# The head of a two-block transformer kernel: first norm ahead of the small vectors, weight loads issued without waiting for them

## The chip, the core and the metric

The kernel runs on one core of a Trainium2 chip. The core has a matrix engine (TensorE, PE in the profile, with its weight loads as PEld), a vector engine (VectorE, DVE), a scalar engine (ScalarE, ACT), GpSimd (POOL) and a sync engine (SyncE, SP) that does nothing here but issue transfers. The engines run their own instruction streams and meet only at semaphores. Sixteen DMA engines move data between the chip's memory (HBM) and the on-chip memory (SBUF). PE writes its results into PSUM, from where DVE or ACT take them; PSUM is used here as eight banks, which the program hands out in rings.

The metric is the device time of one execution in microseconds (us). The numbers compared are medians of several executions.

## What is computed

The reference is a chain of two transformer stacks with 256 tokens of width 1024. Only the beginning matters for this change: the first layer normalizes x and multiplies it with `a_w_in`.

```python
def rmsnorm(x, g):
    xf = x.astype(jnp.float32)
    y = xf * lax.rsqrt(jnp.mean(xf * xf, axis=-1, keepdims=True) + EPS)
    return (y * g.astype(jnp.float32)).astype(x.dtype)
...
def recurrent_block(h, norm_g, w_in, conv_w, conv_b, gate_w, gate_b, lam, w_out):
    u = rmsnorm(h, norm_g)
    z = u @ w_in
    y = jax.nn.gelu(z[..., :LRU_WIDTH])
    xr = causal_conv(z[..., LRU_WIDTH:], conv_w, conv_b)
    hr = rg_lru(xr, gate_w, gate_b, lam)
    return (y * hr) @ w_out
```

Behind it come a gated feed-forward layer, an attention layer with compressed, selected and windowed keys, another feed-forward layer, and then the second stack: two layers with a linear recurrence and a stick-breaking attention, one dense and one mixture-of-experts feed-forward part, and a final norm. All of that is unchanged.

## The kernel before

The whole program is one launch with a hand-written instruction stream for each engine. Weights come through three large slots of SBUF (`raw`, 2 MB each), which SP fills in a fixed order, each load waiting for the last reader of its slot.

The head of the program does this. The x of 256 tokens lies in SBUF as two tiles of 128 tokens (M = 2). The small vectors (norm gains, convolution weights, biases; some of them 8, 16 or 32 rows of 128 numbers) are wanted as columns, one number per partition. They are loaded as rows into `rowbuf`, in two groups: group 0 (8 vectors, 104 rows, a_norm among them) is issued by ACT as its first eight instructions, group 1 (5 vectors, 76 rows) by POOL, all at line 609. PE turns each group with one transpose (`columns`, L625), and DVE copies the result into `cols` (L2099). Semaphores `rows_in[0]` and `rows_in[1]` say that a group has landed.

The norm: ACT squares x and sums each token (L1538), DVE makes the mean (L2009), ACT takes the root (L1540), DVE the reciprocal (L2011) and scales x into `xn` (L2013). PE turns xn with 16 transposes of 128x128 into four PSUM banks (L643), j = 0 and 2 for DVE's ring `me.v` (banks 0 to 2) and j = 1 and 3 for ACT's ring `me.a` (banks 3 to 5). DVE (L2021) and ACT (L1550) bring them to SBUF as `ua`, multiplied with the column of a_norm: so these four need `cols` of group 0. Then PE multiplies ua with the tiles 2 and 3 of `a_w_in` (L658), after it the gates (L744), and later tiles 0 and 1.

Order is set by the order of the code on each engine and by the rings: `claim` waits for a bank to be read before it is written again, `take` waits for it to be filled, `drained` waits until every bank of a ring was read. On PE the order is: columns(0), the 16 transposes, drained, columns(1), the products. On DVE: columns(0), wait for x, the norm, columns(1), then a chain of small instructions on the columns. On SP: load x, load the constants (`const`, the identity matrix of the transposes among them), wait for `rows_in[0]`, and then the weight tiles a_in 2, 3 and 0, for which all three slots are free.

Of the kernel before, what the change touches and what calls it, by code (L numbers as in the profile page):

```python
# [23 lines left out]
P = 128  # L24
S = 256
M = S // P
# [54 lines left out]
def _const_arrays():  # L81
# [44 lines left out]
    for lv in LEVELS + [64]:  # L126
# [9 lines left out]
ROWS = [  # L136
    [("a_norm", 8), ("a_conv_w", 32), ("a_conv_b", 8), ("a_gate_b", 16), ("a_lambda", 8),
     ("kv_norm", 8), ("b_norm", 8), ("f_norm", 16)],
    [("mix_norm_2", 16), ("ffn_norm_2", 16), ("hgrn_lb_logits_2", 8), ("cmp_b1", 4), ("cmp_pos", 32)],
]  # L140
# [6 lines left out]
ROWS_USED = [sum(r for _, r in g) for g in ROWS]  # L147
# [80 lines left out]
def build(nc, A, out, dbg=None):  # L228
    plan, order = weight_plan()
    ctx = ExitStack()  # L230
    with ctx:
# [7 lines left out]
        x = sbuf("x", [P, M, D])  # L239
        xn = sbuf("xn", [P, M, D])  # L240
        with ExitStack() as st:
            uT = sbuf("uT", [P, KD, S], stack=st)
            raw = sbuf("raw", [P, 3, SLOT], stack=st)
# [3 lines left out]
        const = sbuf("const", [P, CONST_F32.shape[1]])  # L247
        cols = sbuf("cols", [P, 2 * P])
# [25 lines left out]
        with ExitStack() as st:  # L274
            rowbuf = sbuf("rowbuf", [P, 2, P], stack=st)
# [338 lines left out]
        def _(pe):  # L614
            me = Side(pe)
# [4 lines left out]

            def columns(g):
                pe.wait_ge(rows_in[g], 16 * len(ROWS[g]))
                b = me.v.claim(pe)
                r = ROWS_USED[g]
                tr(ps[:, b, 0:r], rowbuf[0:r, g, :], const[0:r, 0:r]).then_inc(v_filled, 1)  # L625

            columns(0)

            def drained(ring):

                pe.wait_ge(ring.read, ring.n)

            def norm(split=False):

                src = x if split == "raw" else xn
                if src is xn:
                    me.see(norm_xn, M)
                for j in range(4):
                    ring = me.s if split else (me.v, me.a)[j % 2]
                    b = ring.claim(pe)  # L640
                    for kk in range(2):
                        for m in range(M):
                            t = tr(ps[:, b, (kk * M + m) * P:(kk * M + m + 1) * P],  # L643
                                   src[:, m, (2 * j + kk) * P:(2 * j + kk + 1) * P], ident)
                    t.then_inc(ring.filled, 1)
                for ring in ((me.s,) if split else (me.v, me.a)):
                    drained(ring)

            def released(key, ring):
# [79 lines left out]


            norm()
            columns(1)
            for t in (2, 3):
                arrived(pe, ("a_in", t))
                for c in range(4):
# [738 lines left out]
        def _(act):  # L1474
# [30 lines left out]
                t.then_inc(norm_h, 1)  # L1505

            me.turned = 0

            def out_project(site):

# [24 lines left out]
            def norm(g=None, ready=None):  # L1535

                for m in range(M):
                    fn(xn[:, m, :], x[:, m, :], ACT.Square, accum_out=small[:, m:m + 1]).then_inc(norm_sq, 1)  # L1538
                me.see(norm_ms)
                fn(small[:, 4:6], small[:, 2:4], ACT.Sqrt).then_inc(norm_rt, 1)  # L1540
                if g is None:
                    return
                if ready:
                    ready()
                for j in (1, 3):
                    b = me.a.take(act)
                    for kk_ in range(2):
                        k = 2 * j + kk_
                        for dst, name, off in g:
                            t = fn(dst[:, k, :], ps[:, b, kk_ * S:(kk_ + 1) * S], ACT.Copy, scale=col(name, off + k))  # L1550
                    t.then_inc(a_read, 1)


            norm([(ua, "a_norm", 0)], ready=lambda: act.wait_ge(v_read, 1))
            me.see(lam_abs)
            fn(lam[:, 1, :], lam[:, 0, :], ACT.Exp, scale=-1.0).then_inc(lam_exp, 1)
            me.see(lb_set)
# [1 line left out]
            me.see(lb_set)  # L1559
            fn(bound[:, 1:3], bound[:, 1:3], ACT.Ln).then_inc(lb_done, 1)  # L1560

            act.wait_ge(v_read, 3)
            act.wait_ge(a_read, 2)
            fn(xa[:], ua[:], ACT.Copy).then_inc(uh_ready, 1)
            arrived(act, ("a_in", 0))
# [434 lines left out]
        def _(dve):  # L2000
# [1 line left out]
            v = nc.vector  # L2002
            link = lambda ins: me.link(ins, dve_order)

            def norm(g=None):

                me.norms += 1
                me.see(norm_sq, M)
                v.tensor_scalar(small[:, 2:4], small[:, 0:2], 1.0 / D, EPS, ALU.mult, ALU.add).then_inc(norm_ms, 1)  # L2009
                me.see(norm_rt)  # L2010
                link(v.reciprocal(small[:, 6:8], small[:, 4:6]))  # L2011
                for m in range(M):
                    v.tensor_scalar(xn[:, m, :], x[:, m, :], small[:, 6 + m:7 + m], None, ALU.mult).then_inc(norm_xn, 1)  # L2013
                if g is None:
                    return
                for j in (0, 2):
                    b = me.v.take(dve)
                    for kk_ in range(2):
                        k = 2 * j + kk_
                        for dst, name, off in g:  # L2020
                            t = v.tensor_scalar(dst[:, k, :], ps[:, b, kk_ * S:(kk_ + 1) * S], col(name, off + k), None, ALU.mult)  # L2021
                    t.then_inc(v_read, 1)
# [72 lines left out]
                    low(name, 1, B0, n0)  # L2095

            def columns(g):
                b = me.v.take(dve)
                v.tensor_copy(cols[:, g * P:g * P + ROWS_USED[g]], ps[:, b, 0:ROWS_USED[g]]).then_inc(v_read, 1)  # L2099

            columns(0)
            dve.wait_ge(v_read, me.v.n)
            dve.wait_ge(x_in, 16)


            norm([(ua, "a_norm", 0)])
            columns(1)
            link(v.memset(zp[:, :, 0:CONV - 1], 0.0))

# [846 lines left out]
        def _(sp_eng):  # L2956
# [1 line left out]
            sy.dma_start(x[:], A["x"].rearrange("a (m p) d -> p (a m) d", p=P)).then_inc(x_in, 16)  # L2958
            sy.dma_start(const[:], A["const_f32"]).then_inc(const_in, 16)

            sy.wait_ge(rows_in[0], 16 * len(ROWS[0]))

            def kp(w):
                return w.rearrange("(k p) n -> p k n", p=P)

# [272 lines left out]
```

## Time and profile before

| | us |
|---|---|
| median of 3 runs | 2409.49 |
| lowest and highest | 2406.86, 2411.09 |
| the profiled execution, its own time | 2405.46 |
| its span in the trace (first to last instruction) | 2403.9 |
| mean granted TensorE clock | 0.986 |
| PE busy | 2323.0 (97% of the span) |
| DVE, ACT, POOL busy | 1700.2, 1373.1, 100.5 |

The trace is of one profiled execution; its times are counted from the start of the span. The execution's own time is 1.6 us above the span, and 4.0 us below the median of the three runs.

### The profile page before, as it was taken

The page shows a single profiled execution, that of the slowest core. Times are in us where ns is not written, and L with a number is a line of the kernel's source. Part 1 is how long each engine was busy: PE and PEld are TensorE (multiplying, and loading weights), DVE is VectorE, ACT ScalarE, POOL GpSimd, SP SyncE. Part 2 cuts the span into 40 slices and gives each one's busy share as a digit, 9 for nine tenths or more (in the row PEclk, how much of TensorE's full clock was granted, in tenths as well). Part 3 has the DMA queues.
Part 4 walks back from the last instruction along what each step waited for, and adds up shares of the span by engine and source line. Part 5 has one row for each costly group of instructions (what it writes and reads, how often), then busy time and mean ns, then how long its engine had stood idle before and what let it go on. Part 6 is the DMA issues. An engine that isn't in the chain of part 4 may idle for free.

```text
span 2403.9 us, 31557 instructions
## 1 busy us (share of the span) xinstructions
PE 2323.0 (97%) x12242; PEld 1945.8 (81%) x12242; DVE 1700.2 (71%) x1609; ACT 1373.1 (57%) x1217; POOL 100.5 (4%) x111
## 2 busy tenths in 40 slices
PE   7999999999999999999999989999999999999998
PEld 6888845888889978888999778787878787878786
DVE  6655545655556766545767678888888888888897
ACT  4543303544446855433567456777767676767675
POOL 0000020000001100000011000000000000000020
PEclk9999999999999999999999989999999999999999
DMA  6455363055434236445343399999999999999992
GB/s 233 173 195 209 142 244 126 1 210 210 172 118 176 106 115 255 165 170 205 115 161 121 137 367 409 359 380 352 389 343 382 351 391 352 390 342 380 351 388 109
DMA packets 204633, 588.63 MB, mean 245 GB/s; under 512 B 9164, under 2 KB 17552, under 8 KB 204544
## 3 DMA queue, kind: packets, MB, share of 16 engines
q1 hardware_dynamic: 197696, 564.28, 62.9%
q0 software_dynamic: 6656, 23.04, 2.5%
q8 instruction: 64, 1.05, 0.2%
q14 instruction: 25, 0.20, 0.0%
q10 hardware_dynamic: 192, 0.05, 0.0%
HBM read 573.19 MB, written 14.16 MB: 244 GB/s over the span
## 4 chain that ended last, share of the span: by engine, by line
PE 92%; DVE 4%; ACT 2%; issue 1%; DMA 0%; ACTq 0%; DVEq 0%
PE ps L1385 8%; PE ps L1386 8%; PE ps L1387 8%; PE ps L781 8%; PE ps L783 8%; PE ps L782 8%; PE ps L666 4%; PE ps L1425 4%; PE ps L1424 4%; PE ps L1426 4%; PE ps L676 3%; PE ps L675 3%; PE ps L677 3%; PE ps L658 2%; PE ps L1159 1%
## 5 line engine op out<-in xcount | busy, mean ns | idle before, releaser
L2039 DVE TENSOR_TENSOR more_low<-more_parts,high_parts 128x2048 fp32r<-128x2048 f32 x192 | 432.0, 2288 | 39.3 <-ACT high_parts L1494 38.3
L1494 ACT ACTIVATE high_parts<-more_parts 128x2048 fp32r<-128x2048 f32 x192 | 364.4, 1918 | 109.1 <-PE ps L1387 63.6
L1385 PE MATMUL ps<-high_parts,xmh 128*128 128x512 f32 x896 | 358.1, 400 | 19.5 <-DVE more_low L2039 17.1
L1387 PE MATMUL ps<-high_parts,xml 128*128 128x512 f32 x896 | 353.0, 394 | 0.0
L2039 DVE TENSOR_TENSOR raw_low<-raw,high_parts 128x2048 fp32r<-128x2048 f32 x144 | 323.9, 2286 | 29.5 <-ACT high_parts L1494 29.5
L1494 ACT ACTIVATE high_parts<-raw 128x2048 fp32r<-128x2048 f32 x144 | 275.9, 1921 | 94.3 <-PE ps L1387 51.3
L1609 ACT ACTIVATE wh<-raw 128x4096 fp32r<-128x4096 f32 (+1 forms) x57 | 196.6, 3452 | 190.3 <-PE ps L783 179.8
L2210 DVE TENSOR_TENSOR wl<-raw,wh 128x4096 fp32r<-128x4096 f32 (+1 forms) x57 | 239.2, 4197 | 60.6 <-ACT wh L1609 60.5
L781 PE MATMUL ps<-wh,xh 128*128 128x512 f32 (+1 forms) x632 | 243.9, 386 | 2.1 <-issue 1.5
L783 PE MATMUL ps<-wh,xl 128*128 128x512 f32 (+1 forms) x632 | 239.6, 379 | 0.0
L782 PE MATMUL ps<-wl,xh 128*128 128x512 f32 (+1 forms) x632 | 239.4, 379 | 0.0
L1386 PE MATMUL ps<-more_low,xmh 128*128 128x512 f32 x576 | 227.6, 395 | 0.0
L1385 PEld LDWEIGHTS ps<-high_parts,xmh 128*128 128x128 f32 x896 | 170.6, 190 | 59.6 <-DVE more_low L2039 20.5
L1387 PEld LDWEIGHTS ps<-high_parts,xml 128*128 128x128 f32 x896 | 170.6, 190 | 37.2
L676 PE MATMUL ps<-raw_low,uh 128*128 128x256 f32 x704 | 197.8, 281 | 0.0
L1424 PE MATMUL ps<-high_parts,hh 128*128 128x512 f32 x448 | 175.3, 391 | 2.9 <-DVE hl L2872 1.5
L1426 PE MATMUL ps<-high_parts,hl 128*128 128x512 f32 x448 | 174.2, 389 | 0.0
L781 PEld LDWEIGHTS ps<-wh,xh 128*128 128x128 f32 x632 | 118.9, 188 | 24.7 <-issue 2.1
L783 PEld LDWEIGHTS ps<-wh,xl 128*128 128x128 f32 x632 | 118.9, 188 | 23.1
L782 PEld LDWEIGHTS ps<-wl,xh 128*128 128x128 f32 x632 | 119.0, 188 | 21.0
L676 PEld LDWEIGHTS ps<-raw_low,uh 128*128 128x128 f32 x704 | 132.5, 188 | 0.1
L2485 DVE TENSOR_TENSOR raw_low<-raw,wmh 128x2048 fp32r<-128x2048 f32 x44 | 104.4, 2372 | 34.4 <-ACT wmh L1797 33.5
(545 smaller groups left out, 4452.7 us busy)
## 6 DMA issues: line engine op xcount, KB each, us to landing
more_parts<-in_moe_w_gate SPq DMA_DIRECT2D x78, 1024.0 KB, 5.1
more_parts<-in_moe_w_up SPq DMA_DIRECT2D x66, 1024.0 KB, 7.2
raw<-in_moe_w_down SPq DMA_DIRECT2D x64, 1024.0 KB, 6.0
more_parts<-in_moe_w_down SPq DMA_DIRECT2D x48, 1024.0 KB, 6.4
raw<-in_moe_w_up SPq DMA_DIRECT2D x46, 1024.0 KB, 5.2
raw<-in_w_in SPq DMA_DIRECT2D x22, 2048.0 KB, 7.9
raw<-in_f_w_in SPq DMA_DIRECT2D x20, 2048.0 KB, 8.5
raw<-in_moe_w_gate SPq DMA_DIRECT2D x34, 1024.0 KB, 6.9
```

The source lines that it names most:

```text
L676: mm(o, uh[:, k, ms], wl_[:, k, :], start=False, stop=False)
L781: mm(ps[:, bank, 0:n], xa, a, start=(begin and k == 0), stop=False)
L782: mm(ps[:, bank, 0:n], xa, l, start=False, stop=False)
L783: return mm(ps[:, bank, 0:n], xb, a, start=False, stop=(end and k == last))
L1385: mm(o, xmh[:, k, :], hi[:, cs], start=(k == 0), stop=False)
L1386: mm(o, xmh[:, k, :], lo[:, cs], start=False, stop=False)
L1387: t = mm(o, xml[:, k, :], hi[:, cs], start=False, stop=(k == KD - 1))
L1424: mm(o, ha[:, hs], hi[:, cs], start=(p == 0 and i == 0 and cc == 0), stop=False)
L1426: t = mm(o, hb_[:, hs], hi[:, cs], start=False, stop=(p == 3 and c == 3))
L1494: fn(part_high(j), part_raw(j), ACT.Copy).then_inc(hi_done, 1)
L2039: v.tensor_tensor(part_low(j), part_raw(j), part_high(j).bitcast(F32), ALU.subtract).then_inc(lo_done, 1)
L2210: v.tensor_tensor(wl[:, kind, 0:n], raw[:, plan[name][kind][0], 0:n], wh[:, kind, 0:n].bitcast(F32), ALU.subtract).then_inc(wl_full[kind], 1)
```

## The change

Four things are moved, and nothing is computed otherwise.

- On PE, `columns(0)` and `columns(1)` go from before and behind the norm's transposes to a place behind all 16 of them, ahead of the wait that the rings are read.
- Both take their PSUM banks from another ring, `me.s` (banks 6 and 7), and so are counted by `s_filled` and `s_read`. ACT's count of that ring, which it takes from later, is set to start at 2.
- On DVE, the norm's first part (mean, reciprocal, scaling) comes first, then columns(0) and a wait for it, then the gained copies, then columns(1) as before. ACT waits for `s_read` instead of `v_read` before its own gained copies.
- On SP, the wait for `rows_in[0]` ahead of the first weight tile is gone.

```diff
@@ tensor engine
             def columns(g):
                 pe.wait_ge(rows_in[g], 16 * len(ROWS[g]))
-                b = me.v.claim(pe)
+                b = me.s.claim(pe)
                 r = ROWS_USED[g]
-                tr(ps[:, b, 0:r], rowbuf[0:r, g, :], const[0:r, 0:r]).then_inc(v_filled, 1)
-
-            columns(0)
+                tr(ps[:, b, 0:r], rowbuf[0:r, g, :], const[0:r, 0:r]).then_inc(s_filled, 1)
...
                     t.then_inc(ring.filled, 1)
-                for ring in ((me.s,) if split else (me.v, me.a)):
+                columns(0)
+                columns(1)
+                for ring in (me.v, me.a):
                     drained(ring)
...
             norm()
-            columns(1)
@@ scalar engine
             me.turned = 0
+            me.s.n = len(ROWS)
...
-            norm([(ua, "a_norm", 0)], ready=lambda: act.wait_ge(v_read, 1))
+            norm([(ua, "a_norm", 0)], ready=lambda: act.wait_ge(s_read, 1))
...
-            act.wait_ge(v_read, 3)
+            act.wait_ge(v_read, 2)
@@ vector engine
                     v.tensor_scalar(xn[:, m, :], x[:, m, :], small[:, 6 + m:7 + m], None, ALU.mult).then_inc(norm_xn, 1)
-                if g is None:
-                    return
+                gains_in()
...
-            columns(0)
-            dve.wait_ge(v_read, me.v.n)
+            def gains_in():
+                columns(0)
+                dve.wait_ge(s_read, me.s.n)
+
             dve.wait_ge(x_in, 16)
@@ sync engine
             sy.dma_start(const[:], A["const_f32"]).then_inc(const_in, 16)
 
-            sy.wait_ge(rows_in[0], 16 * len(ROWS[0]))
-
```

How this stands on PE at the start of the program, with what each instruction waits for (rowbuf holds the rows of the small vectors, xn the normalized x, ua the turned and gained x, raw the weight slots). Before:

```order
L625 MATMUL ps<-const,rowbuf 128x104 [waits rows_in0,const_in]
L643 MATMUL ps<-const,xn 128x128 [waits norm_xn]
L643 MATMUL ps<-const,xn 128x128 x15
L625 MATMUL ps<-const,rowbuf 128x76 [waits rows_in1,v_read,a_read]
L658 MATMUL ps<-ua,raw 128x256 [waits v_read,slot_full2]
```

And on PE at the same place in the changed kernel:

```order
L639 MATMUL ps<-const,xn 128x128 [waits norm_xn,const_in]
L639 MATMUL ps<-const,xn 128x128 x15
L625 MATMUL ps<-const,rowbuf 128x104 [waits rows_in0]
L625 MATMUL ps<-const,rowbuf 128x76 [waits rows_in1]
L656 MATMUL ps<-ua,raw 128x256 [waits slot_full2,a_read,v_read]
```

The turn of group 0 moved from the first place to the one behind the transposes of xn, the turn of group 1 no longer waits for the rings, and the first product (L656) waits for the rings itself.

On DVE at the start of the program (small holds the sums, means and roots; cols the columns). Before:

```order
L2099 COPY cols<-ps 128x104 [waits v_filled]
L2009 TENSOR_SCALAR small<-small 128x2 [waits norm_sq,x_in,v_read]
L2011 RECIPROCAL small<-small 128x2 [waits norm_rt]
L2013 TENSOR_SCALAR xn<-x,small 128x1024 [waits dve_order]
L2013 TENSOR_SCALAR xn<-x,small 128x1024
L2021 TENSOR_SCALAR ua<-ps,cols 128x256 [waits v_filled]
```

And on DVE in the changed kernel:

```order
L2007 TENSOR_SCALAR small<-small 128x2 [waits norm_sq,x_in]
L2009 RECIPROCAL small<-small 128x2 [waits norm_rt]
L2011 TENSOR_SCALAR xn<-x,small 128x1024 [waits dve_order]
L2011 TENSOR_SCALAR xn<-x,small 128x1024
L2096 COPY cols<-ps 128x104 [waits s_filled]
L2018 TENSOR_SCALAR ua<-ps,cols 128x256 [waits v_filled,s_read]
```

The copy of group 0's columns moved from ahead of the mean to between the scaling of x and the first gained copy, and that gained copy now waits for it.

On SP at the start of the program, before:

```order
L2958 DMA x<-in_x 128x2x1024
L2959 DMA const<-in_const_f 128x1899
L2972 DMA raw<-in_a_w_in 128x8x512 [waits rows_in0]
L2972 DMA raw<-in_a_w_in 128x8x512 x2
L2972 DMA raw<-in_a_gate_w 128x16x128 [waits v_filled]
```

And on SP in the changed kernel:

```order
L2957 DMA x<-in_x 128x2x1024
L2958 DMA const<-in_const_f 128x1899
L2969 DMA raw<-in_a_w_in 128x8x512 x3
L2969 DMA raw<-in_a_gate_w 128x16x128 [waits v_filled]
```

The three weight tiles stand directly behind x and the constants, with no wait ahead of them.

## Rows read from the trace of the kernel before

**Rows 1.** The page: busy time of each engine, and the chain by engine.

```profile
PE 2323.0 (97%) x12242; PEld 1945.8 (81%) x12242; DVE 1700.2 (71%) x1609; ACT 1373.1 (57%) x1217; POOL 100.5 (4%) x111
...
PE 92%; DVE 4%; ACT 2%; issue 1%; DMA 0%; ACTq 0%; DVEq 0%
```

**Rows 2.** Chain of waits, 0 to 75 us: start, length, what.

```profile
4.06 6.02 DMA rowbuf<-in_f_norm
10.22 0.42 PE ps L625
...
13.07 2.83 PE ps L643 x12
...
17.72 0.26 PE ps L625
17.98 27.84 PE ps L658 x128
```

**Rows 3.** Timeline, 0 to 60 us: start, length, engine, line, what [idle before].

```profile
1.62 0.33 ACTq L609 DMA_DIRECT2D rowbuf<-in_a_conv_w  x1
...
4.06 0.33 ACTq L609 DMA_DIRECT2D rowbuf<-in_f_norm  x1
...
4.42 1.28 ACT L1538 ACT_TABLE_LOAD   x1 [4.42 <-issue]
...
5.88 1.06 ACT L1538 ACTIVATE xn<-x 128x1024 f32<-128x1024 f32 x1 [0.18 <-DMA x<-in_x]
...
8.09 1.28 ACT L1540 ACT_TABLE_LOAD   x1
...
10.66 0.27 DVE L2099 COPY cols<-ps 128x104 f32<-128x104 f32 x1 [10.66 <-PE ps L625]
10.96 0.17 DVE L2009 TENSOR_SCALAR small<-small 128x2 f32<-128x2 f32 x1
11.16 0.20 ACT L1540 ACTIVATE small<-small 128x2 f32<-128x2 f32 x1 [1.79 <-DVE small L2009]
...
13.07 3.67 PE L643 MATMUL ps<-const,xn 128*128 128x128 f32 x16 [2.45 <-DVE xn L2013]
...
15.93 0.88 DVE L2021 TENSOR_SCALAR ua<-ps,cols 128x256 f32<-128x256 f32 x2 [0.83 <-PE ps L643]
16.78 0.84 ACT L1550 ACTIVATE ua<-ps,cols 128x256 f32<-128x256 f32 x2 [0.80 <-PE ps L643]
```

**Rows 4.** Busy time by stretch: length, PE, PEld, DVE, ACT, POOL, PEclk, DMA, GB/s.

```profile
18.00:45.00 27.00, 27.00 (x125) 23.78 (x126) 24.39 (x56) 9.63 (x9) 0.00 (x0) 1.00 0.52 183
45.00:64.00 19.00, 19.00 (x133) 18.04 (x132) 16.32 (x36) 14.03 (x21) 0.00 (x0) 1.00 0.62 222
```

**Rows 5.** Weight issues, 0 to 12 us: issue times ns, then us to landing.

```profile
L2972 SPq DMA_DIRECT2D raw<-in_a_w_in x3: 378/583/3188, 10.1 to 11.1; - x3
...
DMA to landing us min/median/max: 7.8/12.8/17.5
```

**Rows 6.** The constants' load (L2959): issue, then us to landing.

```profile
L2959 SPq DMA_DIRECT2D const<-in_const_f x1: 458/458/458, 1.5 to 1.5; - x1
...
DMA to landing us min/median/max: 7.4/7.4/7.4
```

**Rows 7.** DMA queues, 2.6 to 5.3 us (q1 SP's, q10 ACT's, q0 POOL's).

```profile
q1 hardware_dynamic: 245, 1.00, 90.8%
```

**Rows 8.** DMA queues, 5.5 to 7.5 us.

```profile
q1 hardware_dynamic: 100, 0.76, 90.1%
q10 hardware_dynamic: 89, 0.03, 5.7%
```

**Rows 9.** DMA queues, 7.5 to 8.5 us.

```profile
q1 hardware_dynamic: 28, 0.09, 23.0%
q10 hardware_dynamic: 87, 0.02, 9.6%
```

**Rows 10.** DMA queues, 11 to 14.33 us.

```profile
q1 hardware_dynamic: 470, 0.96, 88.7%
```

More of the change, by code:

```diff
@@ L622, in columns, with norm @@
                 pe.wait_ge(rows_in[g], 16 * len(ROWS[g]))
-                b = me.v.claim(pe)
+                b = me.s.claim(pe)
                 r = ROWS_USED[g]
-                tr(ps[:, b, 0:r], rowbuf[0:r, g, :], const[0:r, 0:r]).then_inc(v_filled, 1)
-            columns(0)
+                tr(ps[:, b, 0:r], rowbuf[0:r, g, :], const[0:r, 0:r]).then_inc(s_filled, 1)
             def drained(ring):
                 pe.wait_ge(ring.read, ring.n)
[L633 to L637, printed above, removed]
+            def norm():
+                me.see(norm_xn, M)
                 for j in range(4):
-                    ring = me.s if split else (me.v, me.a)[j % 2]
+                    ring = (me.v, me.a)[j % 2]
                     b = ring.claim(pe)
@@ L643, in norm @@
                             t = tr(ps[:, b, (kk * M + m) * P:(kk * M + m + 1) * P],
-                                   src[:, m, (2 * j + kk) * P:(2 * j + kk + 1) * P], ident)
+                                   xn[:, m, (2 * j + kk) * P:(2 * j + kk + 1) * P], ident)
                     t.then_inc(ring.filled, 1)
-                for ring in ((me.s,) if split else (me.v, me.a)):
+                columns(0)
+                columns(1)
+                for ring in (me.v, me.a):
                     drained(ring)
@@ L2003, in _, with norm @@
             link = lambda ins: me.link(ins, dve_order)
-            def norm(g=None):
+            def norm(g, gains_in):
                 me.norms += 1
@@ L2097, in columns @@
             def columns(g):
-                b = me.v.take(dve)
-                v.tensor_copy(cols[:, g * P:g * P + ROWS_USED[g]], ps[:, b, 0:ROWS_USED[g]]).then_inc(v_read, 1)
-            columns(0)
-            dve.wait_ge(v_read, me.v.n)
+                b = me.s.take(dve)
+                v.tensor_copy(cols[:, g * P:g * P + ROWS_USED[g]], ps[:, b, 0:ROWS_USED[g]]).then_inc(s_read, 1)
+            def gains_in():
+                columns(0)
+                dve.wait_ge(s_read, me.s.n)
             dve.wait_ge(x_in, 16)
-            norm([(ua, "a_norm", 0)])
+            norm([(ua, "a_norm", 0)], gains_in)
             columns(1)
```

## The prediction, made before the changed kernel had run

> **What bounds the kernel now.** The page comes first. PE is busy for 2323.0 us, 97% of the span, and 92% of the chain that ended last is PE [rows 1]. So a change pays if it lets PE start or go on earlier, and a stall at the head costs its full length if PE is bound from there on. The chain of the first 75 us shows what holds PE at the head: the rows of the small vectors, whose last load (f_norm) is issued at 4.06 and ends 6.02 us later, at 10.08; the turn of group 0 at 10.22; the 16 transposes from 13.07; the turn of group 1 at 17.72; and from 17.98 on the products without a gap for 27.84 us [rows 2]. The stretches behind it show PE full: 27.00 of 27.00 us from 18 to 45, 19.00 of 19.00 from 45 to 64, at a granted clock of 1.00 [rows 4]. A shift of the start at 17.98 therefore goes through to the later stages nearly whole. That is the number to predict: **when does L656, the first product, start in the changed kernel.**
>
> The timeline shows what happens ahead of it. x has landed at 5.88, when ACT begins the squares [rows 3]; at 8.09 they are over and ACT loads the table of the root for 1.28 us, to 9.37. DVE's mean, which needs only the squares, stands behind the copy of group 0 and runs at 10.96, so the root waits until 11.16 [rows 3]. This is the stall the change removes.
>
> **The change part by part.**
>
> *The norm ahead of the rows.* The mean no longer waits for the rows. The squares' last sum is there at about 8.07, the mean takes 0.17, and the root is then held by the table until 9.37: it starts at about 9.40 instead of 11.16 [rows 3]. Gain so far 1.76 us. From the root to the first transpose it is 13.07 - 11.16 = 1.91 us [rows 3], so the transposes start at 9.40 + 1.91 = 11.31. They need the constants, landed at 1.47 + 7.4 = 8.9 [rows 6]; nothing queued behind them on the same queue should hold them up. The 16 transposes end where ACT's last copy starts, 16.78 - 13.07 = 3.71 us later [rows 3]: 15.02.
>
> *The turn of group 0 behind all transposes.* Here most of the gain goes back. In the kernel before, DVE and ACT drain the first three banks while PE still turns; only the last copy (ACT, 0.84 us from 16.78) lies behind [rows 3]. Now all four copies wait for the columns of group 0, which PE turns last. From the start of that turn to DVE's copy of it it is 10.66 - 10.22 = 0.44 us and the copy takes 0.27 [rows 2, 3], with about 0.04 to the next instruction: 15.02 + 0.75 = 15.77. Then DVE and ACT each have two banks, side by side: 2 x 0.88 = 1.76 on DVE, 2 x 0.84 = 1.68 on ACT [rows 3]. Rings drained at 17.53. From the end of ACT's last copy at 17.62 to the next turn on PE at 17.72 it was 0.10 [rows 2, 3]: the first product at **17.63**.
>
> *The turn of group 1* went from 17.72 to 17.98 in the kernel before, 0.26 us behind the drained rings [rows 2]. It now lies at about 15.4, under the copies of DVE and ACT, and costs nothing, if its rows (POOL's queue) are there by 15.4. If they are not, it holds the products one for one.
>
> *The weights without the wait.* The first tile landed 7.8 us after its issue at 10.1, at 17.9 [rows 5], just as the first product started: it would have taken over as the limit at once. Now it is issued at about 2.0 and moves behind the constants, whose last packets pass between 7.5 and 8.5 [rows 9]. At the rate of the stream (470 packets of 2 KB in 3.33 us from 11 to 14.33 with its slow start [rows 10], 190 a us when full) its 1024 packets need 5.4 us: landed at about 14, 3.6 us ahead of its use. So this part gives nothing of its own; without it the rest would give 0.1 us.
>
> *Ring and counts.* The other PSUM ring costs nothing: both turns find its two banks empty. On DVE, some twenty small instructions and the first convolutions follow the copies; they start about 0.4 us earlier, with the products.
>
> Sum: the start goes from 17.98 to 17.63, a gain of 1.76 (root) + 0.26 (group 1) - 1.67 (behind the transposes now 2.51, from 15.02 to 17.53, where 0.84 stood) = **0.35 us**. On the profiled execution's 2405.46 this gives 2405.1. The three runs lie around 2409.49, 4.0 above it, so I put the forecast at 2409.49 - 0.4 = **2409.1**. That is 0.02%; a measurement of this kernel tells about 0.2%, or 4.8 us, from no change.
>
> *Bounds of what the trace does not show.* Two things are not in it: ACT issuing loads while SP is stuck in one, and rows moving beside a stream of weights. For the rows, the near row speaks for little: from 5.5 to 7.5 SP's queue moved 100 packets of the constants (7.6 KB each), ACT's 89 and all of it in turns [rows 8], and ACT's last 87 passed by 8.5 [rows 9]. Between packets of 2 KB they would pass sooner; low end 8.9, no loss. The far row is the one from 2.6 to 5.3: while x moved, 245 packets of SP's queue and none of ACT's [rows 7], though conv_w had been issued at 1.62 [rows 3]. A queue can so shut the others out for 16 packets an engine, 2.7 us. I take landing at 10 to 13 us, nearer the first row because the rows are already waiting when the weights begin; the need is at 15.0, so there is a margin of 2 to 5 us. High end: rows behind both queued tiles, below.
>
> In the Trainium skill, "DMA: Bandwidth & Descriptors", section "Queues, rings and completion order", each DMA engine goes round its queues and drains a packet of some 9 to 17 descriptors from one before it turns to the next. By that rule the rows wait a few turns at most and the forecast stands; the shut-out of about 16 an engine in [rows 7] agrees with it, the mixture in [rows 8] is finer.
>
> **The rivals.**
>
> *ACT is caught behind SP's third tile (slower).* In the kernel before, the three weight issues took 378, 583 and 3188 ns [rows 5]: the third, begun at 11.14, could not end before 470 packets had gone [rows 10], so its queue was full. Nobody else issued then. Now the third issue begins at about 3.0 and by the same count ends when x (256 packets), the constants (128) and 470 of the first tile are gone: 8.0 + 470/190 = 10.5. ACT still has three or four rows to issue after 3.0, the last at 4.06, and its squares stand behind them on the same engine. If what generates the descriptors is shared and stays held by SP, ACT issues them from 10.5 on at 0.4 us each, ends at 12.0 instead of 4.4, and the squares start at 13.3 (with the table load of 1.28 ahead of them) instead of 5.88. Everything follows 7.4 us late: products at 25.0, net loss 7.0 us, **2416.5**. It begins to cost with a hold of 0.2 us (ACT's first table load ends at 5.70, x has landed at 5.88 [rows 3]) and decides from one of about 5.3 us, where 0.35 is eaten and 4.8 lost. For it: the full queue. Against it: ACT's conv_w issue at 1.62 overlapped SP's issue of the constants (1.5 to 1.9) and took its plain 0.33 [rows 3, 6]; but then no queue was full.
>
> The Trainium skill, "Perfetto Trace Analysis", section "DMA Instruction — HWDGE (DVE, Sync)", says that the block that generates descriptors is locked for exclusive use by one sequencer and that the profiled duration begins with the wait for the lock. By that rule ACT's issues from 3.3 us on would read up to some 7 us instead of 0.33, and this rival's time would come true. No row of the kernel before has two engines at that block with a full queue, so the trace does not decide it.
>
> *The rows come behind the weights (slower).* If the engines serve loads as they were issued, the last ones, up to f_norm at 4.06, come behind two tiles: 8.0 + 2080/190 = 18.9, and 1.6 until seen (last packet before 8.5, waiter released at 10.08 [rows 2, 9]): 20.5. Then the turn, the column copy, the two copies and the start take 2.6: 23.1, a loss of 5.1 us; with half of the third tile ahead as well 2.8 more. **2414.6 to 2417.4**. It costs anything only from a landing after 15.0. For it: the rows did land after the constants, which were issued before them. Against it: the turns in [rows 8].
>
> *No gain at all.* If the transposes or copies run slower side by side, 0.2 to 0.5 us vanish and the time is 2409.5. It can't be told from the forecast.
>
> *Faster than 0.2%.* x lands at 5.88 and root, transposes and copies are a chain; with everything else free the start could not go under 16 us. 2 us are 0.08%. Only chance of the measurement gives this.
>
> **How the numbers follow.** Forecast (with the no-gain case) 0.69, ACT caught 0.18, rows behind the weights 0.10, anything else 0.03. The forecast's own range is the spread of the runs, 2406 to 2412. For 8 in 10 the range must take in most of the first rival, so 2405.5 to 2416.8. Faster by over 0.2%: 0.02. Within 0.2% (2404.7 to 2414.3): the forecast 0.69 and a small part of the second rival, 0.71. Slower: 0.18 + 0.08 + 0.01 = 0.27.
>
> **What would show it.** Right: the mean (L2007) at about 8.3, the root at 9.4, the first transpose at 11.3, the turns of the rows at 15.0 and 15.4, the first product at 17.6, and ACT's row issues over at 4.4 with squares at 5.9. ACT caught: row issues of several us, squares after 10. Rows late: a gap on PE behind the transposes that ends with a rowbuf load. Wrong in another way: PE idle again between 18 and 64 us, for then the head is not what sets the later start.

## The result, and the profile after

The change makes the kernel a little slower: 2411.48 us (median of 22 runs, 2407.14 to 2413.93) against 2408.44 us for the kernel before (22 runs beside them, 2404.22 to 2411.09). The ratio is 1.0013, 95% interval 1.0007 to 1.0019, so 3.0 us more, between 1.7 and 4.6. That is under the 0.2% that the prediction set as its bound for "no change", but it is a loss, where a gain of 0.4 us was forecast. The two profiled executions differ by 6.2 us in their spans (2410.1 and 2403.9); single executions of one kernel lie that far apart (2404.22 to 2411.09 for the kernel before), so the spans say nothing by themselves; the head of the trace says where the loss is made.

The chain of waits of the changed kernel, 0 to 75 us (start, length, what), longest pieces:

```profile
1.48 0.46 SPq L2958
1.98 17.36 DMA raw<-in_a_w_in
19.34 0.14 issue
19.48 30.30 PE ps L656 x128
49.77 6.91 PE ps L741 x32
```

Before, the norm's chain set the start of the products at 17.98 and they took 27.84 us [rows 2]. Now a **weight tile** sets it. It was issued at 1.98, 8.1 us earlier than before, and landed at 19.34, 1.4 us later than before (17.9 [rows 5]). And the same 128 records take 30.30 us, 2.46 more. The stretch ends at 49.77 instead of 45.82: 3.95 us, of which 1.50 are the later start and 2.46 slower products. The gates behind it (L741) take 6.91 us in both kernels, and the shift is not taken back: some 250 us later a row of 80 products (L664; L666 in the kernel before) starts at 301.17 instead of 297.25. That fits the 3.0 us (1.7 to 4.6) of the totals.

The timeline of the changed kernel, 0 to 24 us, shows the steps ahead of that:

```profile
2.87 0.61 ACTq L609 DMA_DIRECT2D rowbuf<-in_a_lambda  x1
...
4.29 0.33 ACTq L609 DMA_DIRECT2D rowbuf<-in_f_norm  x1
...
6.03 1.06 ACT L1536 ACTIVATE xn<-x 128x1024 f32<-128x1024 f32 x1
...
8.33 0.17 DVE L2007 TENSOR_SCALAR small<-small 128x2 f32<-128x2 f32 x1 [8.33 <-ACT xn L1536]
9.53 0.20 ACT L1538 ACTIVATE small<-small 128x2 f32<-128x2 f32 x1
...
11.53 3.65 PE L639 MATMUL ps<-const,xn 128*128 128x128 f32 x16 [11.53 <-DVE xn L2011]
14.97 0.51 PE L625 MATMUL ps<-const,rowbuf 104*128 104x104 f32 x2
15.39 0.27 DVE L2096 COPY cols<-ps 128x104 f32<-128x104 f32 x1 [4.00 <-PE ps L625]
15.69 1.57 ACT L1548 ACTIVATE ua<-ps,cols 128x256 f32<-128x256 f32 x4 [5.96 <-DVE cols L2096]
15.69 1.66 DVE L2018 TENSOR_SCALAR ua<-ps,cols 128x256 f32<-128x256 f32 x4
...
19.48 5.03 PE L656 MATMUL ps<-ua,raw 128*128 128x256 f32 x11 [4.00 <-DMA raw<-in_a_w_in]
```

Everything on PE, DVE and ACT up to 17.35 went as forecast within about 0.2 us: both turns of rows from 14.97 on without a wait, the gained copies of both engines over at 17.35. Then PE stands 4.00 us for the weights. The 11 product records listed from 19.48 on take 5.03 us.

### The profile page after: what moved, and what is told of

Read it like the earlier page. It is cut to its first block, busy times and chain, and to the rows that moved or that the text cites. A ratio compares the mean times of both kernels' runs of the same rounds, so it can differ in the third digit from the quotient of the medians.

```text
span 2410.1 us, 31558 instructions
## 1 busy us (share of the span) xinstructions
PE 2327.5 (97%) x12242; PEld 1949.9 (81%) x12242; DVE 1700.0 (71%) x1609; ACT 1372.8 (57%) x1217; POOL 100.4 (4%) x111
## 4 chain that ended last, share of the span: by engine, by line
PE 93%; DVE 4%; ACT 2%; issue 1%; DMA 1%; ACTq 0%; SPq 0%; DVEq 0%
PE ps L1382 8%; PE ps L1383 8%; PE ps L1384 8%; PE ps L778 8%; PE ps L780 8%; PE ps L779 8%; PE ps L664 4%; PE ps L1422 4%; PE ps L1421 4%; PE ps L1423 4%; PE ps L674 3%; PE ps L673 3%; PE ps L675 3%; PE ps L656 2%; PE ps L1157 1%; PE ps L1156 1%
## 5 line engine op out<-in xcount | busy, mean ns | idle before, releaser
L2036 DVE TENSOR_TENSOR raw_low<-raw,high_parts 128x2048 fp32r<-128x2048 f32 x144 | 323.9, 2286 | 27.9 <-ACT high_parts L1491 27.9
L1383 PEld LDWEIGHTS ps<-more_low,xmh 128*128 128x128 f32 x576 | 111.2, 193 | 22.5
```

The source lines that it names most:

```text
L1383: mm(o, xmh[:, k, :], lo[:, cs], start=False, stop=False)
L2036: v.tensor_tensor(part_low(j), part_raw(j), part_high(j).bitcast(F32), ALU.subtract).then_inc(lo_done, 1)
```

## The experiments

Two causes were to be found: why the tile lands late, and why the products then run slowly. Theory A for the first: GpSimd's five broadcasts (`bc`, 344 KB) and the rows share the 16 DMA engines with the weights. Its rivals: the new order of work costs of itself (B), or three queued tiles hold up each other (C). For the second: PE is slow after standing, against disturbance of the products by something else (D). Beside the total, which tells some 2 us from nothing, each run is read by the end of its 128 product records. That number is close to the change, but it comes from one execution of each kernel.

### The wait put back

```diff
             sy.dma_start(const[:], A["const_f32"]).then_inc(const_in, 16)
 
+            sy.wait_ge(rows_in[0], 16 * len(ROWS[0]))
```

> The changed kernel with SyncE's wait for the first group of rows put back; the new order of norm, turns and rings stays. Theory A (the early weights are the whole loss: they share the DMA engines with the broadcasts and rows, so the first tile lands later than when it is issued at 10.1): the tile lands near 17.9 as in the kernel before, the first product starts at 17.9 to 18.0, PE has stood 2.4 us instead of 4.0 ahead of it; time within 1 us of the kernel before, ratio 0.9996 to 1.0008 (the upper end if PE is slow after 2.4 us of standing). Rival B (the new order on PE and DVE costs of itself): ratio about 1.0013 as in the changed kernel.

Ratio 1.0002 (0.9993 to 1.0011), 2408.8 against 2407.64 us. Chain of waits of this run, 0 to 80 us:

```profile
10.31 7.96 DMA raw<-in_a_w_in
18.40 30.71 PE ps L656 x128
```

The tile landed at 18.27 after 7.96 us, about as fast as before (7.8). The total speaks for A, without separating the kernels by much: its interval overlaps that of the changed kernel. The head shows that this version isn't the kernel before in time either: PE's work ended at 15.3, it stood 3.06 us, and the products took 30.71 us. So in this trace the new order brings PE's work forward into a wait for weights that land when they did, and the slow products cost 2.87 us. The stretch ends 3.30 us behind the kernel before, more than the 2.6 us to which the interval of the total reaches; whether every execution of this version pays that much is not shown. The expectation's start (17.9 to 18.0) was 0.4 early.

### Only the wait taken out of the kernel before

```diff
-            sy.wait_ge(rows_in[0], 16 * len(ROWS[0]))
-
```

> The kernel before with only SyncE's wait for the first group of rows taken out. Theory A: the first tile lands at about 19.3 as in the changed kernel, rows land between 10 and 12 and hold the norm as long; the first product starts at 19.4 or later, 1.5 us or more behind the kernel before, ratio 1.0006 to 1.0020. Rival B: no loss, ratio within 1.0004 of 1.

Ratio 1.0011 (1.0002 to 1.002), 2410.99 against 2407.64 us. The timeline of PE, 7 to 27 us:

```profile
10.44 0.41 PE L625 MATMUL ps<-const,rowbuf 104*128 104x104 f32 x1 [10.44 <-DMA rowbuf<-in_f_norm]
13.29 3.68 PE L643 MATMUL ps<-const,xn 128*128 128x128 f32 x16 [2.45 <-DVE xn L2013]
17.94 0.36 PE L625 MATMUL ps<-const,rowbuf 76*128 76x76 f32 x1 [0.97 <-DVE ua L2021]
19.96 7.23 PE L658 MATMUL ps<-ua,raw 128*128 128x256 f32 x20 [1.66 <-DMA raw<-in_a_w_in]
```

The rows came only 0.2 us later than before, the first tile at 19.92, 0.6 later than expected, and the start at 19.96 is as expected. This one line of the change is enough for the late tile and for a loss of the size seen; B falls as the reason for the late tile. That the new order costs nothing isn't shown: with the wait put back, the head had its own 2.87 us of slow products.

### The broadcasts held until the first tile has landed

```diff
             load_rows(po, 1)
+            po.wait_ge(slot_full[2], 16)
             for name, (at, w) in BC.items():
```

> The changed kernel with GpSimd's five broadcast loads (bc, 344 KB) held until the first weight tile has landed. Theory A: without them the stream of weights runs at full rate behind the constants, the first tile lands at 14 to 15, the first product starts at 17.4 to 17.7, at full speed if a stand of 2 us does no harm; ratio to the kernel before 0.9995 to 1.0005. Rival C (the issue of three tiles one behind the other fills the queue and itself spoils the distribution over the 16 DMA engines, broadcasts or not): the tile still lands at about 19.

Ratio 1.0002 (0.9993 to 1.0011). The DMA queues from 8.5 to 14 us (packets, MB, share of the 16 engines), first in the changed kernel, then in this one:

```profile
q1 hardware_dynamic: 451, 0.92, 47.7%
q0 software_dynamic: 169, 0.30, 44.1%
q10 hardware_dynamic: 21, 0.00, 0.4%
```

```profile
q1 hardware_dynamic: 1044, 2.11, 104.8%
q10 hardware_dynamic: 14, 0.00, 0.2%
```

GpSimd's queue (q0) moved 0.30 MB in 169 packets, and SyncE's queue (q1) moved 593 packets less in the same 5.5 us. Without the broadcasts the tile landed 12.3 us after its issue at 1.98, at 14.3, and its stream ran at the 190 packets a us that the prediction had counted on (1044 in 5.5 us). In the chain of waits of this run PE starts when its own chain allows, and at full speed:

```profile
17.33 27.89 PE ps L656 x128
45.23 6.91 PE ps L741 x32
```

17.33 against the forecast's 17.63, and the end of the stretch is 0.59 us ahead of the kernel before. So the prediction's sum for the head comes true as soon as the broadcasts are out of the way. The total (2408.32 against 2407.64 us) can't tell it from no change.

### More transposes while PE waits

```diff
                 columns(1)
+                for _ in range(17):
+                    tr(ps[:, 2, 0:P], xn[:, 0, 0:P], ident)
                 for ring in (me.v, me.a):
```

> The changed kernel with 17 more transposes on PE, into a PSUM bank that the first product overwrites, in the stretch in which PE waits for the first tile (added work, no result used). Theory A with the slow start: the first product starts at 19.5 as in the changed kernel, but the 128 product records of the first stretch take 27.8 us instead of 30.3, and the whole is 2.4 us faster than the changed kernel, ratio to the kernel before about 1.0003. Rival D (the slow products come from something else, such as DMA writes into the weight slots at the same time): still 30.3 us, ratio 1.0013.

Ratio 1.0 (0.9991 to 1.0009). The timeline of PE, 7 to 27 us, and the chain of waits:

```profile
11.63 3.61 PE L639 MATMUL ps<-const,xn 128*128 128x128 f32 x16 [11.63 <-DVE xn L2013]
15.07 0.33 PE L625 MATMUL ps<-const,rowbuf 104*128 104x104 f32 x2
15.24 2.02 PE L645 MATMUL ps<-const,xn 128*128 128x128 f32 x17
```

```profile
19.49 27.86 PE ps L658 x128
47.36 6.91 PE ps L743 x32
```

The start is the same 19.49, the weights arrive as late, and the products take 27.86 us: D falls. The total went with it, 1.0 against the changed kernel's 1.0013, and not the 1.0003 expected. The row of the added transposes says more: 17 in 2.02 us, where the 16 ahead of them took 3.61. PE worked at half rate until about 15 and at full rate from then on, and the products were fast behind the 2.23 us that were left to wait.

### Only the first tile early

```diff
                 if kind == "a_in":
+                    if t == 3:
+                        sy.wait_ge(slot_full[2], 16)
```

> The changed kernel with only the first weight tile issued early; the other two are issued once it has landed. The broadcasts stay early. Theory A (the broadcasts' own packets and the weights' packets share the DMA engines, whatever is queued behind): the first tile lands at 16 to 19.5. Rival C (three tiles queued one behind the other hold up the generation of descriptors, so that engines run dry): the first tile lands at 13 to 15.

The chain of waits of this run:

```profile
1.98 17.57 DMA raw<-in_a_w_in
```

The first tile landed 17.57 us after 1.98, at 19.55, with no weights queued behind it. C falls. This kernel ran once, 2413.69 us beside a median of 2406.72, and nothing is concluded from that total.

### The broadcasts twice, and all but one

```diff
             for name, (at, w) in BC.items():
                 po.dma_start(bc[:, at:at + w], flat_view(A[name]).partition_broadcast(P)).then_inc(bc_in, 16)
+                po.dma_start(th[:].rearrange("p k s -> p (k s)")[:, at:at + w],
+                             flat_view(A[name]).partition_broadcast(P)).then_inc(bc_in, 16)
```

The waits for the broadcasts further on (DVE's for `bc`, and one more on ACT ahead of a write of `th`) count the doubled loads; they are not printed here.

> The changed kernel with each of GpSimd's five broadcasts issued a second time, into a buffer that is free at that time (added transfers of 344 KB, no result used). Theory A: the first tile, which lost about 5 us to one set (14.3 without, 19.3 with), loses more to two: it lands at 22 to 25. Rival C: it lands at 19 to 20 as before.

```diff
             for name, (at, w) in BC.items():
+                if name == "hgrn_out_norm_2":
+                    po.wait_ge(slot_full[2], 16)
```

> The changed kernel with only the last and largest broadcast (hgrn_out_norm, 128 of the 344 KB) held until the first tile has landed. Theory A, cost by bytes: the tile lands about 37% of the way from 19.3 to 14.3, at about 17.5; cost by the number of loads: one of five, at about 18.3.

The chains of waits, of the version with two sets and of the one with the largest held:

```profile
1.98 22.98 DMA raw<-in_a_w_in
25.09 30.35 PE ps L656 x128
```

```profile
1.98 16.16 DMA raw<-in_a_w_in
18.28 30.55 PE ps L656 x128
```

The tile lands at 14.3 with no broadcast, at 18.14 with the first four (216 KB), at 19.34 with all five (344 KB), at 24.96 with two sets (688 KB). A second set costs 5.6 us where the first cost 5.0. By bytes the four should have cost 3.2 us, by number of loads 4.0; they cost 3.8, nearer to the number of loads (or of their packets) than to the bytes. That is one trace each, and in the four kernels with all five broadcasts early the tile landed anywhere from 19.34 to 19.92, so the difference of 0.6 us between the two is a hint and no more. Each ran once, 2417.44 and 2408.21 us.

### Broadcasts late, and group 0 turned ahead of the transposes

On top of the held broadcasts, PE's order is put back to that of the kernel before, while DVE keeps the norm first:

```diff
+            columns(0)
             norm()
...
-                columns(0)
                 columns(1)
```

> The changed kernel with two further edits: GpSimd's five broadcasts are held until the first weight tile has landed, and PE turns the first group of rows ahead of the 16 transposes (the rows are there at about 10.4, the transposes begin at 11.4). Theory A: the tile lands at 14.3 and PE's copies no longer wait behind the turn, so the copies of the first three banks lie beside the transposes and only the last one behind: the last copy ends at about 16.0, the first product starts at 16.1, 1.9 us ahead of the kernel before and 1.2 ahead of the run with late broadcasts alone; at full speed, 27.9 us for the 128 records. End of that stretch at 44.0. Ratio to the kernel before 0.9985 to 1.0001. If the chain is held by something else, the first product starts at 17.3 as with late broadcasts alone.

Ratio 0.9998 (0.9989 to 1.0007); the medians, 2407.21 and 2406.72 us, lie the other way round, and neither tells it from no change. The timeline of PE, 7 to 27 us, and the chain:

```profile
11.71 3.68 PE L639 MATMUL ps<-const,xn 128*128 128x128 f32 x16 [0.96 <-DVE xn L2011]
15.18 0.33 PE L625 MATMUL ps<-const,rowbuf 76*128 76x76 f32 x1
```

```profile
16.36 30.27 PE ps L655 x128
```

The start went to 16.36, 1.6 us ahead of the kernel before, and was lost again: the expectation had 27.9 us for the products, and missed. PE had stood only 0.85 us, and they still took 30.27 us. So it isn't the length of the stand alone.

### Short fillers behind, and behind and ahead

```diff
+            for _ in range(6):
+                tr(ps[:, 2, 0:P], ident, ident)
             columns(0)
+            for _ in range(4):
+                tr(ps[:, 2, 0:P], ident, ident)
             norm()
...
                 columns(1)
+                for _ in range(5):
+                    tr(ps[:, 2, 0:P], xn[:, 0, 0:P], ident)
```

The first run has the last five only, the second all fifteen.

> The last version with late broadcasts and group 0 turned early, whose first product started at 16.4 but whose 128 product records took 30.3 us, with 5 more transposes on PE behind the turn of group 1, without use of their result, in the 0.85 us in which PE stood. If it was that stand that left PE slow: records of 380 ns from the start, 27.9 us for the 128, end of the stretch at 44.2. If PE had not yet been fast when the transposes ended (they began at 11.7, and take 421 ns a record in every run so far): the five take 421 ns a record too, and the products are slow at least at first, end at 44.2 to 46.6. Ratio to the kernel before 0.9985 to 1.0005.

> The same with 10 more transposes of the identity ahead of the norm's, from the landing of the constants at 8.9 on, around the turn of group 0 (no result used). PE is at work from 8.9 on instead of 11.5. Expected: the later ones of the norm's 16 transposes already take 272 ns a record instead of 421, the 16 need 2.0 to 3.0 us instead of 3.65, the first product starts at 15.3 to 16.1, records of 380 ns from the start, end of the 128 at 43.2 to 44.0, 1.8 to 2.6 us ahead of the kernel before; ratio 0.9985 to 0.9998. If work ahead of the norm doesn't make PE faster: transposes at 421 ns, start at 16.3.

Five behind: ratio 0.9992 (0.9983 to 1.0001), 2405.79 against 2407.48 us. All fifteen: **0.9987 (0.9977 to 0.9996)**, 2405.03 against 2407.48 us, the only version whose interval lies below 1; it overlaps that of the version with five. The chains of waits:

```profile
11.44 3.68 PE ps L639 x16
16.09 27.86 PE ps L657 x128
43.96 6.91 PE ps L743 x32
```

```profile
14.99 27.86 PE ps L657 x128
42.86 6.91 PE ps L747 x32
```

And the timeline of PE of the second, 7 to 27 us:

```profile
9.01 1.54 PE L731 MATMUL ps<-const 128*128 128x128 f32 x6 [9.01 <-DMA const<-in_const_f]
10.73 0.44 PE L625 MATMUL ps<-const,rowbuf 104*128 104x104 f32 x1 [0.17 <-DMA rowbuf<-in_f_norm]
10.96 1.06 PE L734 MATMUL ps<-const 128*128 128x128 f32 x4
11.81 2.21 PE L639 MATMUL ps<-const,xn 128*128 128x128 f32 x16
```

The 16 transposes take 2.21 us instead of 3.65, and the products start at 14.99 at full speed, 0.3 us ahead of the expected 15.3 to 16.1. The stretch ends 2.96 us ahead of the kernel before; the medians differ by 2.45. In the version with five, the five took 0.72 us from 15.04 on (273 ns a record, not 421), so PE was fast by then, the first of the two outcomes expected, and it stood 0.34 us instead of 0.85.

### All runs beside each other

"Tile" is the landing of the first weight tile, "start" and "128 records" are of the first products, "end" is their end, in us of each trace; "stood" is how long PE had nothing to do right ahead of them (in the kernel before: ahead of the turn of group 1, which passes into the products).

| kernel | tile | stood | start | 128 records | end | ratio to the kernel before |
|---|---|---|---|---|---|---|
| before | 17.9 | 0.97 | 17.98 | 27.84 | 45.82 | |
| changed | 19.34 | 4.00 | 19.48 | 30.30 | 49.77 | 1.0013 |
| wait put back | 18.27 | 3.06 | 18.40 | 30.71 | 49.12 | 1.0002 |
| before, wait taken out | 19.92 | 1.66 | 19.96 | 30.54 | 50.51 | 1.0011 |
| broadcasts late | 14.3 | 1.93 | 17.33 | 27.89 | 45.23 | 1.0002 |
| transposes in the wait | 19.35 | 2.23 | 19.49 | 27.86 | 47.36 | 1.0 |
| one tile early | 19.55 | 4.39 | 19.68 | 30.57 | 50.25 | one run |
| broadcasts twice | 24.96 | 9.60 | 25.09 | 30.35 | 55.44 | one run |
| largest broadcast late | 18.14 | 2.88 | 18.28 | 30.55 | 48.83 | one run |
| late, group 0 early | 14.4 | 0.85 | 16.36 | 30.27 | 46.63 | 0.9998 |
| the same, 5 fillers | 14.4 | 0.34 | 16.09 | 27.86 | 43.96 | 0.9992 |
| the same, 15 fillers | 14.5 | 0.36 | 14.99 | 27.86 | 42.86 | 0.9987 |

## Why the prediction was wrong

**The norm ahead of the rows: right.** Root at 9.53 (forecast 9.40), transposes at 11.53 (11.31), their length 3.65. Most of the 0.13 to 0.22 us too much is there from the start: the squares begin at 6.03 instead of 5.88.

**The turns behind the transposes: right.** The turns from 14.97 on, group 1 without a wait, copies over at 17.35 (17.53), since two of them took 1.66 us and not 1.76. With the tile there, the products started at 17.33 (17.63), as the run with late broadcasts shows.

**The weights without the wait: wrong, and this is the step that failed.** The prediction took the rate of a stream that was alone (190 packets a us [rows 10]) for a stretch in which GpSimd's queue was at work: "landed at about 14, 3.6 us ahead of its use". The trace of before had a row that speaks against it, the DMA queues from 8.5 to 10 us, when nothing but GpSimd's loads moved:

```profile
q0 software_dynamic: 93, 0.18, 80.3%
```

0.18 MB in 93 packets took 80.3% of sixteen engines, 0.21 us a packet: for these 1.5 us the stretch into which the weights were to move was already nearly full. The prediction asked what the weights do to the rows, and not what GpSimd's loads do to the weights. The term came to 17.36 us from issue to landing, against 12.3 without broadcasts and some 12 in the forecast. Its sentence "this part gives nothing of its own" holds only for the run with late broadcasts; with the broadcasts the late tile cost 1.50 us of start.

**PE's rate: missing altogether.** The prediction looked at the granted clock, 1.00 in all rows [rows 4], and priced only the start; it put the rate of the products at that of before without a reason. The second cost, 2.46 us, comes from what PE did, or did not do, ahead of the products, as the added transposes show; it is larger than the first. The same omission makes its bound wrong that "the start could not go under 16 us": with fifteen fillers it came at 14.99, because the norm's transposes ran faster. The column reads 1.00 also in the stretch in which records take twice as long: busy time by stretch of the changed kernel (length, PE, PEld, DVE, ACT, POOL, PEclk, DMA, GB/s), 15.5 to 49.7 us:

```profile
15.50:19.40 3.90, 0.00 (x0) 0.00 (x0) 3.16 (x15) 3.67 (x8) 0.00 (x0) 1.00 1.05 402
19.50:24.50 5.00, 5.00 (x12) 4.01 (x13) 1.53 (x9) 2.69 (x3) 0.00 (x0) 1.00 1.05 387
24.50:49.70 25.20, 25.20 (x119) 22.18 (x118) 22.04 (x38) 5.00 (x3) 0.00 (x0) 1.00 0.27 90
```

Twelve records in 5.00 us (2.4 a us), then 119 in 25.20 (4.7 a us), half the rate and then the full one. I read this as the lower of TensorE's two levels, 1.2 GHz, and then the upper, 2.4 GHz; it is read from the rate of the records, since the granted clock doesn't show it.

**Rival "ACT is caught behind SP's third tile": did not happen, and was not put to the test as stated.** SyncE's second and third issue in the changed kernel, from its timelines of 2.5 to 4 and of 4.9 to 6 us:

```profile
2.45 2.45 SPq L2969 DMA_DIRECT2D raw<-in_a_w_in  x1
4.94 10.81 SPq L2969 DMA_DIRECT2D raw<-in_a_w_in  x1
```

The third began at 4.94 and not at about 3.0, when ACT's last issue was over (4.29 + 0.33 = 4.62), so no issue of ACT ran beside the 10.8 us. What ran beside SyncE's second issue of 2.45 us took 0.61 us (a_lambda, 0.36 before) and 0.33 to 0.37 (the three behind it, as before). In the run with one tile early, with no issue of SyncE beside it, a_lambda took 0.54 us too, so even these 0.25 us are not shown to be a wait for SyncE's issue. The Trainium skill ("Perfetto Trace Analysis", section "DMA Instruction — HWDGE (DVE, Sync)") has an exclusive lock on the block that generates descriptors, and names VectorE and SyncE as the pair that shares it. By that rule ACT's issues would have waited for the end of SyncE's 2.45 us; they did not, and here the measurement decides. The case of a longer issue is open.

**Rival "the rows come behind the weights": did not happen.** The turns ran at 14.97 without a wait, and where PE waited for the rows (wait taken out of the kernel before) the turn began at 10.44 instead of 10.22. So the rows were not held behind the weights that were queued ahead of them. The rule of the Trainium skill ("DMA: Bandwidth & Descriptors", section "Queues, rings and completion order"), by which an engine goes round its queues, agrees with that. The same turns went to the broadcasts, 169 packets of GpSimd's queue beside 451 of SyncE's from 8.5 to 14 us, and that is what hurt.

**The numbers.** 2411.48 lies in the range of 2405.5 to 2416.8, and in "within 0.2%", which had 0.71; but the direction is the other one, and none of the named mechanisms brought it. That the range held is luck: its room was for a rival that didn't come.

What stays open: what exactly decides whether PE is fast at a given moment. The products were fast after a stand of 0.34 to 0.97 us in three kernels, and of 1.93 and 2.23 us; they were slow after 2.88 us and more in all five kernels that had it, but also after 1.66 us (wait taken out of the kernel before) and 0.85 us (group 0 turned early). No simple limit on the stand gives this. The turns of the rows show more, because their record is longer at the lower rate. Group 0's, shortly ahead of the stand, first in the changed kernel, then with one tile early (groups of PE's instructions, 11 to 19 us: busy us, mean ns, idle us before):

```profile
L625 PE MATMUL ps<-const,rowbuf 104*128 104x104 f32 x1 | 0.4, 381 | 0.0
L625 PE MATMUL ps<-const,rowbuf 104*128 104x104 f32 x1 | 0.3, 255 | 0.0
```

Both kernels had given PE the same work up to there, begun at 11.53 and 11.57, and one had PE slow at 15.0, the other fast. In the same way group 1's turn took 0.26 us in the kernel before and 0.36 with the wait taken out, after the same work and the same stand of 0.97 us. So the level doesn't follow from PE's own work alone, as far as the traces show it, and a head may be slow in one execution and fast in the next. With late broadcasts the turns were as slow as in the changed kernel (381 and 334 ns), PE then stood 1.93 us, and the products were fast: PE was raised in between, while it stood. With one tile early it was fast at 15.0 and slow after 4.39 us: it was lowered there. With group 0 turned early the last turn took 334 ns, so PE had not been raised when it stood. Nor was it tried how the 16 engines share the broadcasts between them, or what the same bytes would cost as a load of SyncE's or ACT's queue; the profile has no view of a single DMA engine.

## What to carry to other kernels

Before a large load is moved forward, look at every queue that is at work in the stretch it is moved into, the small ones of other engines too: here small loads didn't only wait for a large one, they also slowed it, and by more than their bytes. If the consumer ends up waiting for the load, count the start of its work and its rate apart, and move what nobody needs yet (here 344 KB of broadcasts) behind what somebody waits for. A matrix engine that is idle ahead of a long dense stretch can be given a few transposes without use; here fifteen moved the end of the first products by 3.8 us (46.63 to 42.86), where late broadcasts and all reordering together had moved it by 0.8 the wrong way.

## What the runs showed of the hardware

- Five broadcasts to 128 partitions, 344 KB in all, took 5.0 us from a stream of weights that runs at 380 to 400 GB/s alone, where their bytes at that rate would be 0.9 us. Their packets, 1.8 KB on average (0.30 MB in 169), held an engine for 0.23 us each in the changed kernel (44.1% of 16 engines for 5.5 us over 169), against 0.088 for packets of 2 KB of the weights alone (104.8% over 1044).
- In those 5.5 us the engines were 92% busy by their shares (47.7 + 44.1 + 0.4) and moved 1.22 MB, against 2.11 MB with weights alone.
- TensorE's slow stretch: records at half rate for about 5 us, 2.4 to 2.9 us lost in seven of the twelve kernels here. Transposes of 128 columns took 0.23 us each at the lower rate and 0.12 at the upper. The granted clock of the profile read 1.00 in the rows of both. The Trainium skill, "TensorE: Matmul & The Clock Gate", section "Part 1: The HAM clock gate (the "warmup" mystery)", has an idle array at the lower level and a busy one at the upper. The fillers agree, and the five long stands; the slow products behind stands of 0.85 and 1.66 us, and the raising of PE within a stand of 1.93 us, are not settled by that sentence.
- An issue on SyncE behind two others took 10.8 us (15.7 with two sets of broadcasts, 5.7 with the broadcasts late); I take its queue to have been full. The issues of ScalarE that ran beside SyncE's one of 2.45 us took 0.33 to 0.61 us.
